# Compressed attention branch: token blocks laid out by GpSimd, block-diagonal keys, gate products moved ahead

## What is computed

```python
blk_idx = jnp.arange(n_cmp)[:, None] * 16 + jnp.arange(32)[None, :]   # n_cmp = 31
def compress(t, pe, w1, w2):
    blocks = t[:, :, blk_idx] + pe
    flat = blocks.reshape(B, G, n_cmp, 32 * 64)
    return jax.nn.gelu(flat @ w1) @ w2
kc = compress(k_cmp, pe_k, wk1, wk2)
vc = compress(v_cmp, pe_v, wv1, wv2)
s_c = jnp.einsum('bghsd,bgnd->bghsn', qh, kc) * scale
```

## Time and profile before

| | us |
|---|---|
| median of 3 runs | 2882.46 |
| lowest and highest run | 2877.77, 2885.74 |
| span of the profiled execution | 2882.1 |
| its own time, as far as reported (no run is named as the profiled one; the median lies 0.4 above the span) | 2882.5 |
| PE busy | 2723.4 (94%) |
| DVE, ACT, POOL busy | 1475.0 (51%), 1214.8 (42%), 365.1 (13%) |
| stretch from the gates' last product to the start of the first nsa job | 205.2 to 286.6 |

### The profile page before, as it was taken

The page is one execution under the profiler, slowest core; times in us unless marked ns, Lnnn a source line. Parts: engine busy times, 40 slices in busy tenths (PEclk is TensorE's granted clock), DMA queues, the critical chain, the costliest instruction groups (busy, mean ns, idle before and its releaser), DMA issues. The chain is left out here.

```text
span 2882.1 us, 51525 instructions
## 1 busy us (share of the span) xinstructions
PE 2723.4 (94%) x22200; PEld 2148.3 (75%) x22200; DVE 1475.0 (51%) x2357; ACT 1214.8 (42%) x2071; POOL 365.1 (13%) x310
## 2 busy tenths in 40 slices
PE   8999999999989999999889999899898988899999
PEld 6877557788878888776478888677677775688887
DVE  3533775744353333445744243596677785543343
ACT  4322663632242222324634233375566665432232
POOL 0001550000000000001200000000444543000000
PEclk9999999999999999999999999899999998899999
DMA  4222002233222222232122222222000001322221
GB/s 180 95 71 88 1 1 95 73 132 111 97 81 107 94 103 103 81 130 70 52 93 99 103 88 102 102 74 89 10 9 8 7 8 34 117 102 96 102 97 64
DMA packets 38801, 228.50 MB, mean 79 GB/s; under 512 B 4352, under 2 KB 8448, under 8 KB 15024
## 3 DMA queue, kind: packets, MB, share of 16 engines
q1 hardware_dynamic: 32576, 201.34, 19.6%
q0 software_dynamic: 6000, 23.87, 2.4%
HBM read 220.93 MB, written 4.26 MB: 78 GB/s over the span
## 5 line engine op out<-in xcount | busy, mean ns | idle before, releaser
L446 DVE TENSOR_TENSOR weights_lo<-ring,weights_hi 128x1024 fp32r<-128x1024 f32 x359 | 441.6, 1233 | 696.1 <-ACT weights_hi L439 695.9
L439 ACT ACTIVATE weights_hi<-ring 128x1024 fp32r<-128x1024 f32 x364 | 382.6, 1053 | 575.0 <-PE bank L576 335.3
L495 PE MATMUL bank<-mlp_h_hi,weights_hi 128*128 128x512 f32 x384 | 151.2, 394 | 2.0 <-DVE mlp_h_lo L791 2.0
L496 PE MATMUL bank<-mlp_h_lo,weights_hi 128*128 128x512 f32 x384 | 150.8, 393 | 0.0
L497 PE MATMUL bank<-mlp_h_hi,weights_lo 128*128 128x512 f32 x384 | 150.8, 393 | 0.0
L495 PE MATMUL bank<-h_hi,weights_hi 128*128 128x512 f32 x384 | 150.1, 391 | 0.0
L574 PE MATMUL bank<-weights_hi,mlp_p_hi 128*128 128x512 f32 x384 | 149.6, 390 | 0.0
L496 PE MATMUL bank<-h_lo,weights_hi 128*128 128x512 f32 x384 | 149.5, 389 | 0.0
L576 PE MATMUL bank<-weights_hi,mlp_p_lo 128*128 128x512 f32 x384 | 149.4, 389 | 0.0
L575 PE MATMUL bank<-weights_lo,mlp_p_hi 128*128 128x512 f32 x384 | 149.4, 389 | 0.0
L497 PE MATMUL bank<-h_hi,weights_lo 128*128 128x512 f32 x384 | 149.4, 389 | 0.0
(11 more groups left out here) (672 smaller groups left out, 6775.2 us busy)
## 6 DMA issues: line engine op xcount, KB each, us to landing
ring<-in_w_m SPq DMA_DIRECT2D x64, 1024.0 KB, 4.5
ring<-in_w_mb SPq DMA_DIRECT2D x24, 1024.0 KB, 4.5
ring<-in_w_fi SPq DMA_DIRECT2D x22, 1024.0 KB, 4.6
ring<-in_w_fo SPq DMA_DIRECT2D x10, 1024.0 KB, 4.8
ring<-in_w_a SPq DMA_DIRECT2D x7, 1024.0 KB, 4.9
attn_bias<-scratch POOLq DMA_DIRECT2D x16, 448.0 KB, 4.7
ring<-in_w_rg SPq DMA_DIRECT2D x5, 1024.0 KB, 4.9
ring<-in_w_v SPq DMA_DIRECT2D x4, 1024.0 KB, 10.9
```

The lines of the kernel that those rows point to most:

```text
L439: act.e.activation(halves(g, s)[0], raw, ACT.Copy).then_inc(*act.up("act_unit_high", ("high", s)))
L446: lane.e.tensor_tensor(lo, raw, hi.bitcast(F32), ALU.subtract).then_inc(*lane.up(f"{lane.name}_unit_low", ("low", s)))
L495: pe.e.matmul(ps[:, :], hi, xh, start=k == 0, stop=False, skip_group_check=True)
L496: pe.e.matmul(ps[:, :], hi, xl, start=False, stop=False, skip_group_check=True)
```

## The change

- POOL adds the position term to the token windows and lays them out (`pool_windows`, 16 instructions of 128 x 248), so that the 4 x 31 columns of every position pair stand side by side. They are written over the x area. The fifth block, its memsets and ACT's bias copies are gone. L1079 reads 124 adjacent columns.
- The compressed keys go into a zeroed buffer of 62 columns a group: the even head's keys in rows 0 to 63, the odd head's in rows 64 to 127. One matmul of depth 128 and 62 columns scores two heads, into one bank for every query tile; DVE adds the mask for 16 heads at once.
- The gates' product stands before block 7 of w_kv, and its copy on DVE behind block 6.
- ACT's first three units of w_vt move behind the first job's exponentials; POOL's low parts of them get a function of their own behind the windows.

```diff
-    L.kc2, L.vc2 = three(own[:, 0:5 * S], S), L.yC[:, 3:8, :]
+    L.kc2, L.vc2 = three(own[:, 0:4 * S], S), L.yC[:, 4:8, :]
+    L.windows = [x_area[:, j * 16 * 4 * NCMP:(j + 1) * 16 * 4 * NCMP].rearrange("p (j g n) -> p j g n", g=4, n=NCMP) for j in range(2)]
...
-    L.kc, L.peb = a.take(4 * NCMP), a.take(4)
+    L.kc = a.take3(4, 2 * NCMP)
@@ def pe_nsa_in(g, pe):
-    pe_gemm(g, pe, "w_kv", NB, range(8), part_of(L.hs), lambda nb, k: ())
+    pe_gemm(g, pe, "w_kv", NB, range(7), part_of(L.hs), lambda nb, k: ())
...
     m.then_inc(*pe.up("pe_gates", ("filled", "gates")))
+    pe_gemm(g, pe, "w_kv", NB, range(7, 8), part_of(L.hs), lambda nb, k: ())
@@ def act_nsa_in(g, act):
-    for s in first_units("w_vt"):
-        act_unit(g, act, s)
@@ def dve_nsa_in(g, dve):
-    drain_copy(g, dve, "gates", L.gT[0:48, :], filled(g, dve, "gates")[0:48, :])
+            if i == 6:
+                drain_copy(g, dve, "gates", L.gT[0:48, :], filled(g, dve, "gates")[0:48, :])
@@ def pool_nsa_in(g, pool):
-    for q in (L.kc2, L.vc2):
-        pool.e.memset(q[:, 4, :], 0.0).then_inc(*pool.up("pool_zero"))
-    pool.wait_ge(pool.newest)
-    for q, name in ((L.kc2, "pe_k"), (L.vc2, "pe_v")):
-        pool.e.tensor_copy(q[:, 4, 0:32:2], g.vec[name]).then_inc(*pool.up("pool_positions", ("positions",)))
-    for s in first_units("w_vt"):
-        low_unit(g, pool, s)
+    pool.e.memset(L.kc, 0.0).then_inc(*pool.up("pool_zero", ("kc_zero",)))
+    for kind, (src, name) in enumerate(((L.kc2, "pe_k"), (L.vc2, "pe_v"))):
+        for half in range(2):
+            pool.wait_ge(g.at("drained", ("w_kv", 2 * kind + half)))
+            for grp in (2 * half, 2 * half + 1):
+                pool_windows(g, pool, kind, grp, src[:, grp, :], g.vec[name])
     end(g, pool, "nsa_in")
+def pool_windows(g, pool, kind, grp, src, positions):
+    pairs = src.rearrange("p (n j e) -> p e j n", j=8, e=2)[:, 0]
+    for half in range(2):
+        pool.e.tensor_tensor(g.L1.windows[kind][:, 8 * half:8 * half + 8, grp, :], pairs[:, :, half:half + NCMP],
+                             positions[:, 8 * half:8 * half + 8].unsqueeze(2).broadcast_to((P, 8, NCMP)), ALU.add).then_inc(
+            *pool.up("pool_windows", ("windows", kind)))
@@ def pe_compress(g, pe):
-    pe.wait_ge(g.at("positions"))
...
-        for nb in (2 * kind, 2 * kind + 1):
-            pe.wait_ge(g.at("drained", ("w_kv", nb)))
+        pe.wait_ge(g.at("windows", kind))
...
-                m = pe.e.matmul(ps[:, 0:5 * NCMP].rearrange("p (a b) -> p a b", b=NCMP), w[j], src[:, :, 2 * j:2 * j + 481:16],
-                                start=j == 0, stop=j == 15, skip_group_check=True)
+                m = pe.e.matmul(ps[:, 0:4 * NCMP], w[j], L.windows[kind][:, j].rearrange("p g n -> p (g n)"), start=j == 0,
+                                stop=j == 15, skip_group_check=True)
...
-        banks = [bank(g, pe, ("cmp", qt, par)) for par in range(2)]
+        ps = bank(g, pe, ("cmp", qt))
         for hh in range(8):
-            for par in range(2):
-                rows = slice(64 * par, 64 * par + 64)
-                m = pe.e.matmul(banks[par][:, hh * NCMP:(hh + 1) * NCMP], L.qT[rows, hh, qt * P:(qt + 1) * P],
-                                L.kc[rows, (hh // 2) * NCMP:(hh // 2 + 1) * NCMP], start=True, stop=True, skip_group_check=True)
+            m = pe.e.matmul(ps[:, 2 * hh * NCMP:2 * (hh + 1) * NCMP], L.qT[:, hh, qt * P:(qt + 1) * P], L.kc[:, hh // 2, :],
+                            start=True, stop=True, skip_group_check=True)
@@ def act_compress(g, act):
-        act.e.activation(L.peb[:, c:c + 1], ps[:, 4 * NCMP:4 * NCMP + 1], ACT.Copy).then_inc(*act.up("act_peb"))
-        act.wait_ge(act.newest)
...
     for i in range(3):
         act_nsa_exps(g, act, 0, i)
+    for s in first_units("w_vt"):
+        act_unit(g, act, s)
@@ def dve_compress(g, dve):
+    dve.wait_ge(g.at("kc_zero"))
+    keys = ps[0:64, 0:4 * NCMP].rearrange("p (a b) -> p a b", b=NCMP)
+    drain_copy(g, dve, "kc", L.kc[0:64, :, 0:NCMP], keys, last=False)
+    drain_copy(g, dve, "kc", L.kc[64:128, :, NCMP:2 * NCMP], keys, ("kc_ready",))
...
+        ps = filled(g, dve, ("cmp", qt))
+        dve.e.tensor_tensor(L.Pc[:, qt], ps[:, 0:16 * NCMP].rearrange("p (a b) -> p a b", b=NCMP),
+                            L.cneg[:, qt, :].unsqueeze(1).broadcast_to((P, 16, NCMP)), ALU.add).then_inc(
+            *dve.up("dve_drained", ("drained", ("cmp", qt)), ("cmp", qt)))
+def pool_compress(g, pool):
+    for s in first_units("w_vt"):
+        low_unit(g, pool, s)
+    end(g, pool, "compress")
```

More of the change, by code:

```diff
@@ L1066, in pe_compress @@
     g.rotating = HEADS_ROT
-    pe.wait_ge(g.at("positions"))
     for kind in range(2):
         name = ("wk1", "wv1")[kind]
-        src = (L.kc2, L.vc2)[kind]
-        for nb in (2 * kind, 2 * kind + 1):
-            pe.wait_ge(g.at("drained", ("w_kv", nb)))
+        pe.wait_ge(g.at("windows", kind))
         for hb in range(2):
@@ L1102, in pe_compress @@
     for qt in range(QT):
-        banks = [bank(g, pe, ("cmp", qt, par)) for par in range(2)]
+        ps = bank(g, pe, ("cmp", qt))
         for hh in range(8):
-            for par in range(2):
-                rows = slice(64 * par, 64 * par + 64)
-                m = pe.e.matmul(banks[par][:, hh * NCMP:(hh + 1) * NCMP], L.qT[rows, hh, qt * P:(qt + 1) * P],
-                                L.kc[rows, (hh // 2) * NCMP:(hh // 2 + 1) * NCMP], start=True, stop=True, skip_group_check=True)
-        m.then_inc(*pe.up("pe_cmp", ("filled", ("cmp", qt, 0)), ("filled", ("cmp", qt, 1))))
+            m = pe.e.matmul(ps[:, 2 * hh * NCMP:2 * (hh + 1) * NCMP], L.qT[:, hh, qt * P:(qt + 1) * P], L.kc[:, hh // 2, :],
+                            start=True, stop=True, skip_group_check=True)
+        m.then_inc(*pe.up("pe_cmp", ("filled", ("cmp", qt))))
     pe_token_gemm(g, pe, "w_vt", 1, lambda k: cols(L.hs, k), lambda k, q: ())
@@ L1118, in act_compress @@
         ps = filled(g, act, ("hid", c))
-        act.e.activation(L.peb[:, c:c + 1], ps[:, 4 * NCMP:4 * NCMP + 1], ACT.Copy).then_inc(*act.up("act_peb"))
-        act.wait_ge(act.newest)
-        act.e.activation(L.hid[:, c, 0:4 * NCMP], ps[:, 0:4 * NCMP], ACT.Gelu_apprx_tanh, bias=L.peb[:, c:c + 1]).then_inc(
+        act.e.activation(L.hid[:, c, 0:4 * NCMP], ps[:, 0:4 * NCMP], ACT.Gelu_apprx_tanh).then_inc(
             *act.up("act_hidden", ("hidden", c), ("drained", ("hid", c))))
@@ L1140, in dve_compress @@
     ps = filled(g, dve, "kc")
-    drain_copy(g, dve, "kc", L.kc[0:64, :], ps[0:64, 0:124], last=False)
-    drain_copy(g, dve, "kc", L.kc[64:128, :], ps[0:64, 0:124], ("kc_ready",))
+    dve.wait_ge(g.at("kc_zero"))
+    keys = ps[0:64, 0:4 * NCMP].rearrange("p (a b) -> p a b", b=NCMP)
+    drain_copy(g, dve, "kc", L.kc[0:64, :, 0:NCMP], keys, last=False)
+    drain_copy(g, dve, "kc", L.kc[64:128, :, NCMP:2 * NCMP], keys, ("kc_ready",))
     for i in range(3):
@@ L3324, in pool_program @@
     pool_nsa_in(g, pool)
+    pool_compress(g, pool)
     pool_nsa(g, pool)
```

## The result

| | before | after |
|---|---|---|
| median, us | 2880.11 (4 runs) | 2857.05 (4 runs) |
| lowest to highest | 2877.46 to 2885.74 | 2856.75 to 2859.44 |
| span of the profiled execution | 2882.1 | 2857.7 |

The ratio is 0.9911, with a 95% interval of 0.9899 to 0.9924: 23 us less in the medians, 24.4 in the two profiled spans. Forecast were 2853.3 and a range of 2847 to 2861. A run's time stands 1.7 us above the span of its own profile (2859.44 and 2857.7 here), not 0.4 as the forecast had it, and the profiled execution of the kernel after is the slowest of its four.

A forecast was written before the change was run, and what follows sets the result against it. PE, busy 94% of the span, was taken as the bound; gains 1.0 + 19.7 + 6.6 + 1.9 = 29.2 off the span of 2882.1 gave 2852.9, plus 0.4 for the median 2853.3 us, range 2847 to 2861.

The forecast's parts named there:

- gates ahead of block 7: Before the hidden products: block 7's matmuls hide DVE's copy of the gates, so PE does not wait; gain 1.0 us.
- hidden products: L1079: 128 instructions of 124 adjacent columns at 111 ns, 14.2 us for 33.9; gain 19.7 us.
- kc to the end of the scores: Score matmuls at 62 ns, bounds 56 and 110; w_vt starts 12.0 us after kc's start, not 18.6; gain 6.6 us.
- w_vt at full clock: Start of w_vt: without the half-height 31-column matmuls the clock does not fall; gain 1.9 us.
- rest of the kernel: From w_vt on: all engines keep order and distances, so all of the gain arrives at the end.
- Rival 1: Hidden products: only the number of columns counts, 211 ns each, gain 6.9 instead of 19.7, 2866.1 us; chance 0.08.
- rival 3: Hidden products and scores: full-height loads and passes do not overlap, 164 and 110 ns, 2861.4 us; chance 0.04.
- The new wait that I forecast: Before w_vt: PE idle 1.6 us for POOL's first low part, there 11.95 us after kc's start.
- rival 2: Before w_vt: the clock falls anyway in the new idle stretch, 2855.2 to 2857.1 us; chance 0.18.
- The windows: POOL's 16 additions: 0.64 to 0.99 us each, 2.0 if the step costs; done before PE needs them, cost nothing.
- Rival 4: Hidden products: PE waits for POOL's late windows; 28.8 us lost at 4.8 us each, 2901 at 6; chance 0.04.
- The transfers: Weights: wv1's second piece lands after 4.9 us with 2.1 us slack; w_vt's pieces by 221.5, before ACT wants them.

The follow-up runs named there:

- e11: Kernel after with block 7 of w_kv put back in front of the gates' product; span 2862.0 us.
- e4: Kernel after with the hidden products reading kc2 and vc2 with the step of 16 tokens, four blocks of 31, position term left out; span 2870.4 us.
- e3: Kernel after with the hidden products taking two of four groups, 62 adjacent columns for 124; 112 ns between starts.
- e2: Kernel after with score matmuls on rows 0 to 63 only, all 62 columns; span 2862.7 us.
- e1: Kernel after with score matmuls taking only the even head's 31 key columns, weights still 128 by 128; span 2861.6 us.
- e9: Kernel after with only the first 64 of 128 queries as weights in each score matmul; 60 ns between starts in the scores.
- e5: Kernel after with scores again as pairs of half-height, 31-column matmuls into two banks per query tile; ratio to the kernel before 0.9933.
- e6: Kernel before with only the block-diagonal keys and one bank per query tile added; ratio to the kernel before 0.9985, 4.3 us faster.
- e8: Kernel after with vc in bank 6 and the first query tile's scores in bank 7; median 2856.51 us, ratio 0.9910.
- e7: Kernel after with ACT's first three units of w_vt put back in front of the GELUs; span 2862.0 us.
- e10: Kernel after with the hidden products using only the first 64 of 128 weight columns, 124 moving columns kept; 107 ns between starts.

## Why the prediction was right, point by point

| step | forecast | measured |
|---|---|---|
| gates ahead of block 7 | 1.0 | 0.9 |
| hidden products | 19.7 | 19.4 |
| kc to the end of the scores | 6.6 | 5.1 |
| w_vt at full clock | 1.9 | 1.9 |
| sum up to the nsa stage | 29.2 | 27.3 |
| rest of the kernel | 0 | -2.7 |
| front, before the change | 0 | -0.2 |
| between the two profiled spans | 29.2 | 24.4 |

*Gates.* Right; e11 shows the 0.9 by itself.

*Hidden products.* The front's rows carried over: 113 ns for a forecast of 111. That the step was the cost, argued from the clock's indifference, is borne out by e4, but for the blocks of 31. Rival 1 (columns alone, 211 ns) and rival 3 (164 ns) are out. But the reason for scaling with the columns was not sound: e3 shows that 62 columns cost as much as 124. The number was right in part by luck, because 124 moving and 128 weight columns are nearly equal.

*The scores: the step that failed.* "I take 62, a little over a load of 56 beside a pass of 54." The 56 ns were read from pairs in two row halves, and taken for the cost of one load. They were half of a pair's. A load of 128 float32 columns takes 111 ns at 64 rows (e2) as at 128 (e1), and the loads of the two halves run side by side. L831's own rows would have allowed it: a load of 111 beside a pass of 111 fits them just as well as one of 56. The stage took 7.17 us instead of 4.0, 112 ns each, just over the upper bound of 110 that I had given. Half of the miss was hidden, since w_vt would have waited for POOL until kc + 11.95 in any case (e9): the term fell short by 13.46 - 12.0 = 1.5 us. The new wait that I forecast was therefore real, but not the last to end.

*The third rival's reading.* It had 110 ns in the scores, which came true, but by load and pass in line, and that would have given 83 ns in e1 and 164 in the hidden products. Of the rule of the Trainium skill (TensorE: Matmul & The Clock Gate, "Part 3: Packing small matmuls — row/col tiling") the trace bears out one half and not the other: tiles in different rows do run side by side, loads too (111 ns a pair), but a load also overlaps a matmul in the same rows (in e9 one start every 58 to 60 ns, for a load of 56 and a pass of 54 by theory F).

*The clock.* w_vt ran at full clock, for the reason given: e5 and e6 tie the fall to the half-height, 31-column matmuls, so rival 2 is out there. A low clock came later instead, from 269.11 on, where 16 matmuls of the nsa stage took 3.41 us; e3, e4, e8 and e11, with the same order of work there, have none. The PE instructions from there on are the same in both kernels; counted back from the last, the 20,300th starts at 375.5 before and 349.6 after, a lead of 25.9 for the 27.1 at the end of w_vt.

*Nothing given back later?* Between the two profiled executions 2.7 us were. 1.2 are that fall. The other 1.5 come and go: the lead of 25.9 holds to 700 us, is down to 21.3 at 2100 and stands at 24.4 from 2600 on, with falls of the clock that lie a little otherwise. The order of the work is the same there, and no new wait of PE stands in the nsa stage. The same count in other runs goes either way, and mostly with the clock (all in us):

| run | low clock after 300 us | lead at the end of w_vt | at the end |
|---|---|---|---|
| after | 119.4 | 27.1 | 24.4 |
| e3 | 122.2 | 27.6 | 21.4 |
| e5 | 108.6 | 20.4 | 24.4 |
| e7 | 115.5 | 20.1 | 20.1 |
| e8 | 115.6 | 28.8 | 28.8 |
| e11 | 132.6 | 26.8 | 20.1 |

The kernel before has 115.5. With as much low clock as that, e7 and e8 give nothing back. e3 and e11 lose some 6.5 us at one place, a fall of 13.7 us at 2045 that the other four and the kernel before do not have. Why the clock falls there in one execution and not in another stays open. The times can't tell either: the interval of the ratio, 0.9899 to 0.9924, is 22 to 29 us, which holds 27.1 as well as 24.4.

*How near the time came.* The gain was forecast as 29.2 and is 24.4 between the traces, 23.1 in the medians. The time of 2857.05 lies in the range because the range was drawn wide enough for rival 3 and a high run. It lies 3.7 above 2853.3, while the profiled span lies 4.8 above the 2852.9 forecast for it: the difference is chance, since the profiled execution is the slowest of four.

*The windows* took 0.96 us each, in the stated 0.64 to 2.0, and cost nothing. Rival 4 is out. *The transfers* of wv1 and w_vt were in time, though w_vt's took 6.8 us for the 4.9 assumed; e7 shows what a late one would do.

## What to carry to other kernels

A rate read from instructions that take turns in two row halves is the rate of the pair; before it is used for one full-height instruction, ask which part of it runs side by side. When a "full" engine keeps its pace at half its clock, look at its operand's layout: here that was worth 19.4 of the 27.3 us, more than all waits around it. A stage that gets shorter brings the next producer forward on paper: work out when each input lands, as for the units here, and move what stands in front of it before it becomes the wait.

## What the runs showed of the hardware

- A float32 matmul instruction with 128 weight columns, in the rows of the one before it, starts 111 to 113 ns after it at clock 1.00: with 31 (e1), 62, 124 (after) or 128 moving columns, with 64 (e2) or 128 rows (213 at 0.50, e1 and e2). Two of 64 rows in different halves take the same 111 together. With 64 weight columns and 62 moving ones it is 58 to 60 ns (e9), with 64 and 124 it is 107 (e10).
- A moving operand read with a step of 16 float32, in blocks of 31, costs 1.7 ns a column in place of 0.87: 214 ns for 124 columns (e4), 265 for 155, the latter at both levels of the clock.
- POOL adds 248 elements in 0.96 us when one input is read with that step, 3.9 ns an element; its products of 512 adjacent elements (L2949) have 2.6.
- DVE's product of two inputs of 8 elements took 2.01 us beside POOL's subtraction and ended with it, 0.17 without it (e7).
